# Gate and later-round placement of a mixture-of-experts stage, moved behind the first expert's up product

## What is computed

```python
for e in range(16):                       # 16 SwiGLU experts of width 512
    h = silu(t @ w1[e]) * (t @ w3[e])     # up
    out += gates[:, e:e+1] * (h @ w2[e])  # down
```

## Time and profile before

| | us |
|---|---|
| median of 3 runs | 1329.08 |
| profiled execution, its time | 1333.09 |
| its span (first to last instruction) | 1331.4 |
| PE busy | 910.7 (68%) |
| DVE busy | 416.6 (31%) |
| POOL busy | 312.1 (23%) |
| ACT busy | 171.4 (13%) |
| bytes moved by DMA | 275.74 MB, 207 GB/s over the span |

### The profile page before, as it was taken

How to read it: one execution, slowest core, us unless ns; L and a number is a source line. 1 busy time by engine, 2 the same in 40 slices (tenths; PEclk the granted TensorE clock), 3 DMA queues, 4 the chain that set the end, 5 groups by cost and what they waited for, 6 DMA issues and landing times.

```text
span 1331.4 us, 13807 instructions
## 1 busy us (share of the span) xinstructions
PE 910.7 (68%) x4042; PEld 460.2 (35%) x4043; DVE 416.6 (31%) x887; ACT 171.4 (13%) x316; POOL 312.1 (23%) x568
## 2 busy tenths in 40 slices
PE   3934405969677876873698886669778778766770
PEld 2723302454222322221465653335363223222220
DVE  1599977161111111112412432220531111111114
ACT  1100003030111100100112322111020011101000
POOL 0499995001111211112300001210011211111110
PEclk9967756957999888897699988889859988988886
DMA  7318201085998999995703011217334799999982
GB/s 219 96 32 284 94 0 32 0 290 170 363 363 285 317 361 367 375 373 178 263 12 119 9 36 59 64 36 277 133 102 143 254 356 367 367 378 364 359 298 87
DMA packets 131710, 275.74 MB, mean 207 GB/s; under 512 B 8940, under 2 KB 35800, under 8 KB 131653
## 3 DMA queue, kind: packets, MB, share of 16 engines
q1 hardware_dynamic: 116400, 236.11, 49.7%
q0 software_dynamic: 7808, 20.98, 6.7%
q10 hardware_dynamic: 7461, 18.13, 4.1%
HBM read 257.88 MB, written 18.03 MB: 207 GB/s over the span
## 4 chain that ended last, share of the span: by engine, by line
PE 36%; DMA 33%; DVE 9%; POOL 7%; issue 7%; SPq 3%; ACT 2%; ACTq 2%; POOLq 0%; DVEq 0%
DMA w<-in_e_w 31%; POOL dbuf L420 6%; PE bank L847 5%; PE bank L783 3%; PE wide L847 3%; PE bank L857 3%; PE wide L783 2%; PE bank L1447 2%; PE bank L1348 1%; PE wide L819 1%; PE bank L1327 1%; DVE w L970 1%; PE bank L1499 1%; SPq L1188 1%; DMA x_tok<-sum_rows 1%
## 5 line engine op out<-in xcount | busy, mean ns | idle before, releaser
L847 PE MATMUL bank<-w,dbuf 128*64 128x512 f32 x576 | 145.8, 664 | 44.7 <-DMA w<-in_e_w 42.0
L847 PE MATMUL wide<-w,dbuf 128*64 128x512 f32 x512 | 131.6, 673 | 52.5 <-DMA w<-in_e_w 52.5
L857 PE MATMUL bank<-w,dbuf 128*64 128x512 f32 x544 | 137.2, 649 | 20.5 <-DVE dbuf L1129 19.5
L963 DVE SCALAR_TENSOR_TENSOR w<-w,dw_T x240 | 133.1, 630 | 0.0
L389 POOL TENSOR_TENSOR spare<-spare 1x1 f32<-1x1 f32 x68 | 15.7, 230 | 466.0 <-DVE dbuf L1136 402.8
L847 PEld LDWEIGHTS bank<-w,dbuf 128*64 128x64 f32 x576 | 44.6, 153 | 142.8 <-issue 129.7
L847 PEld LDWEIGHTS wide<-w,dbuf 128*64 128x64 f32 x512 | 41.0, 155 | 142.6 <-issue 138.9
L455 POOL DMA_DIRECT2D w<-in_cache_kpe x64 | 35.4, 553 | 220.9 <-PE bank L1502 174.0
L1136 DVE COPY dbuf<-bank 64x512 f32<-64x512 f32 x64 | 44.0, 688 | 135.7 <-PE bank L857 135.3
L857 PEld LDWEIGHTS bank<-w,dbuf 128*64 128x64 f32 x544 | 45.3, 149 | 87.2 <-issue 85.8
L420 POOL TENSOR_TENSOR dbuf<-dbuf 128x128 f32<-128x128 f32 x124 | 75.0, 605 | 0.3
(11 more groups left out here) (298 smaller groups left out, 1224.1 us busy)
## 6 DMA issues: line engine op xcount, KB each, us to landing
w<-in_e_w SPq DMA_DIRECT2D x96, 2048.0 KB, 14.2
dbuf<-in_a_w_pw SPq DMA_DIRECT2D x16, 512.0 KB, 5.2
w<-in_cache_ckv SPq DMA_DIRECT2D x64, 128.0 KB, 2.3
dbuf<-in_a_w_pw SPq DMA_DIRECT2D x1, 4096.0 KB, 15.1
dbuf<-in_b_w_o SPq DMA_DIRECT2D x1, 4096.0 KB, 12.6
dbuf<-in_b_w_uq SPq DMA_DIRECT2D x1, 3072.0 KB, 12.1
x_rows<-x_tok ACTq DMA_DIRECT2D x4, 512.0 KB, 3.0
dbuf<-in_b_w_dq SPq DMA_DIRECT2D x1, 2048.0 KB, 28.6
```

Of the source, the lines that this page charges most:

```text
L847: last = nc.tensor.matmul(bank[n * C:(n + 1) * C], x[:, k], w[:, n, k], start=(k == 0), stop=(k == KD - 1))
L857: last = nc.tensor.matmul(bank[n * C:(n + 1) * C], h[:, k], w[:, k, n * 512:(n + 1) * 512], start=(k == 0), stop=(k == 3))
L963: V.scalar_tensor_tensor(chunk(acc, j, 0, SEQ), chunk(ext, j, k, SEQ), w, chunk(acc, j, 0, SEQ), ALU.mult, ALU.add).then_inc(tap, 1)
```

## The change

The five calls of line 823 to 827 become a function `gates()`, called behind the first expert's up product. To have a place for the call, expert 0 is written out ahead of the loop and expert 13 behind it; the loop covers experts 1 to 12 with the buffers' parity exchanged. No other engine's program changes.

```diff
--- before.py
+++ after.py
@@ -820,11 +820,14 @@
                 return last
 
             to_slots(B[7][0:C, 0:E], hot, lambda n, m: right[0:m, n, 0]).then_inc(r_slot, 1)
-            pe.wait_ge(r_gated, l + 1)
-            for q in range(CHUNKS):
-                last = to_slots(B[3][0:C, 2 * E * q:2 * E * (q + 1)], hot if q == 0 else hot_more[:, q - 1],
-                                lambda n, m: right[0:m, n].rearrange("p a e -> p (a e)"))
-            last.then_inc(r_gates, 1)
+            def gates():
+
+                pe.wait_ge(r_gated, l + 1)
+                for q in range(CHUNKS):
+                    last = to_slots(B[3][0:C, 2 * E * q:2 * E * (q + 1)], hot if q == 0 else hot_more[:, q - 1],
+                                    lambda n, m: right[0:m, n].rearrange("p a e -> p (a e)"))
+                last.then_inc(r_gates, 1)
+
             g0 = E * l
 
             def turn_rows(bank, src, n):
@@ -890,17 +893,28 @@
 
             n = 16 * (E // 2) * l
             turn(g0, 0, n + 16)
-            with pe.Fori(0, (E - 2) // 2) as it:
+            do_up(g0, 0, 2 * n + 32)
+            gates()
+            turn(g0 + 1, 1, n + 16)
+            pe.wait_ge(cnt_set, l + 1)
+            do_hidden(g0)
+            do_down(g0, 0, n + 16)
+            further(0, 0)
+            with pe.Fori(0, (E - 4) // 2) as it:
                 for s in range(2):
-                    e = it * 2 + s
-                    do_up(e + g0, s, it * 32 + (2 * n + 32))
-                    turn(e + (g0 + 1), 1 - s, it * 16 + (n + 16 + 16 * s))
-                    if s == 0:
-                        pe.wait_ge(cnt_set, l + 1)
+                    e = it * 2 + (s + 1)
+                    do_up(e + g0, 1 - s, it * 32 + (2 * n + 32 + 32 * s))
+                    turn(e + (g0 + 1), s, it * 16 + (n + 32))
                     do_hidden(e + g0)
-                    do_down(e + g0, s, it * 16 + (n + 16))
-                    further(e, s)
-            n += 16 * (E - 2) // 2
+                    do_down(e + g0, 1 - s, it * 16 + (n + 16 + 16 * s))
+                    further(e, 1 - s)
+            n += 16 * (E - 4) // 2
+            do_up(g0 + E - 3, 1, 2 * n + 32)
+            turn(g0 + E - 2, 0, n + 32)
+            do_hidden(g0 + E - 3)
+            do_down(g0 + E - 3, 1, n + 16)
+            further(E - 3, 1)
+            n += 16
             do_up(g0 + E - 2, 0, 2 * n + 32)
             turn(g0 + E - 1, 1, n + 16)
             do_hidden(g0 + E - 2)
```

## The result

The changed kernel took 1346.42 us (median of 7 runs, 1340.87 to 1351.54), the kernel before 1334.58 us (median of 7, 1327.82 to 1337.15). The ratio is 1.011 (95% interval 1.0079 to 1.0141), which is not formed from the two medians: slower by 11.8 us by the medians and by 14.7 us by the ratio. A second measurement of the same kernel gave 1.0064 (1.0035 to 1.0094), 8.5 us, and 11.4 us between the medians. The forecast was +14.2 us.

What follows compares the result with a forecast made beforehand. PE's serial work between slots and expert 1's up product was taken to bound each stage's start, before the weight stream; +8.5 and +5.7 us, together +14.2, on 1329.08 gave 1343.3 us, range 1334 to 1349.

Steps and rivals of the forecast that it cites:

- What bounds: Both expert stages: PE's work between the slots and expert 1's up product is paid in full; weight loads move with it.
- Rival 3: Expert 2's weight landing ends last anyway and absorbs the change: no change, 1329.1 us; chance 0.07.
- rival 4: The 60 products fall into PE's wait between up product and hidden turn: -7.6 us, 1321.5 us; chance 0.03.
- The turn: Turn of expert 0's rows starts earlier, limited by the gather's landing: -2.4 us in layer 0, -5.2 in layer 1.
- The up product: Expert 0's up product stays at 10.07 us; 1.5 us less if the clock rises after 3.05 us.
- Rival 2: Clock not granted in the up product, as PE idles before it: +4.0 us a layer, 1351.3 us; chance 0.06.
- The 60 products: Behind the up product they take 7.3 us a layer, the higher clock lasting 2.9 us; bounds 5.6 and 9.2.
- rival 1: Clock stays high behind the up product, gates 5.6 us a layer, down product not cooled: +5.6, 1334.7 us; chance 0.12.
- The tail: Behind the 60 products: VectorE's lines 1.2 us, table load and loop entry 1.5, silu and gating 1.65 as before.
- Hidden turn and down product: Expert 0's hidden turn and down product run colder after the small products: +0.7 and +0.2, +0.9 us a layer.
- Sum: Later start of expert 1's up product: +8.5 us in layer 0, +5.7 in layer 1, together +14.2 us.
- The base: Median of the runs, 1329.08 us, 4.0 below the profiled 1333.09; the increment was put on it, giving 1343.3 us.

Runs made afterwards that it cites:

- the new loop: Kernel before with expert 0 ahead of PE's loop, expert 13 behind, parity exchanged, but the 60 products still ahead of the first turn: 1334.02 us, ratio 1.0008.
- the early silu: Changed kernel with expert 0's silu and the copy of expert 1's turned rows ahead of ScalarE's count wait: 1344.86 us, ratio 1.0087 to the kernel before.
- the doubled products: Changed kernel with each layer's 60 products run twice behind the up product: 1372.06 us, ratio 1.0266 to the kernel before.
- the split kernel: Against the kernel before: three calls ahead of the first turn, one before and one after the hidden turn, silu ahead of the count wait: 1326.72 us, ratio 0.9937.
- the run with the products in between: Changed kernel's loop form, with the 60 products between expert 0's turn and its up product: 1342.55 us, ratio 1.0053 to the kernel before.

## Why the prediction was right or wrong

*What bounds:* right. What was put into the start interval came out in the measured time, to within some 4 us (the new loop and the early silu had 4 us less in it and were not measurably faster). Rival 3 (the weight stream absorbs it) is out by the doubled products, and rival 4 (the products fall into waiting time) by the 2.92 us in which PE still waits behind them. In the split kernel the products do fall into waiting time, but there by design.

*The turn:* -2.4 and -5.2 were forecast; measured from the slot products it came 1.75 and 5.3 us earlier. The size in layer 0 depends on the gather, which took 7.2 us from issue to landing there and not 6.6. That the wait costs by itself is shown by the run with the products in between.

*The up product:* unchanged at 10.07 forecast. It took 9.1 and 9.9 us, 8.6 and 9.9 in the second trace: in layer 0 it was 0.9 to 1.4 us shorter, by less time at the lower clock, as it also was in the third trace of before (9.26). Rival 2 did not happen.

*The 60 products:* mis-sized. I had 7.3 us, with the clock falling after 2.9; it lasted through nearly all of them, and they took 5.91 and 5.79 us. That is near the 5.6 got from the ratio of 0.61, and not the 3.7 estimated in rival 1. The fall I had read in the earlier trace rows came after 2.9 us in which PE stood idle for half (0.85 and 0.61 us), and I took it over to products without gaps. Rival 1 was right in this and wrong in the rest, as the down product was cold nevertheless.

*The tail:* 1.2 + 1.5 + 1.65 = 4.35 us forecast, 4.28 measured in each layer. The table load began 0.19 us after the count, and silu 0.02 us after the load. The Trainium skill, "ScalarE: Activation LUTs", What ACT_TABLE_LOAD costs, has about 1.38 us of drain with each switch to another table set. Here nothing of that size is seen, and the measurement decides. Nor is it seen where ScalarE was busy until the load, as in the trace of before, whose load begins at 309.46, 0.02 us behind this copy of the turned rows:

```profile
308.84 0.60 ACT L639 ACTIVATE dbuf<-bank 128x512 f32<-128x512 f32 x1 [18.25 <-PE bank L834]
```

The run with the early silu took 2.15 us of the 4.28 away. That load and silu were in PE's path is thus shown, not only argued.

*Hidden turn and down product:* +0.9 a layer forecast against the trace of before. Hidden turn 0.97 and 0.98 against 0.59; down 5.58 and 6.02 against 5.30 and 5.22. Summed that is +0.7 and +1.2, right against that trace; but it was one in which the down product of before was cold in both layers. Against a warm one (3.65) it is +2.3 and more.

*Sum:* the terms give +8.5 and +5.7; the start intervals of the same two traces +6.4 and +4.2. The forecast increment of 14.2 us was thus 3.6 too large in its own terms. Of that the 60 products are 2.9 and the up product of layer 0 is 0.9. In the other direction, the rest of the profiled execution, which I had put at nothing, was 7.9 us longer (attention and experts, cause open). That the increment still lies at the measured 11.8 (medians) to 14.7 (ratio) is in part luck: the two errors have opposite signs.

*The base:* the step that failed. I put the increment on 1329.08, the median of three runs. The kernel before measured 1334.58 us (median of seven) together with the changed one, 5.5 us more, and 1332.2 to 1334.6 later. The changed kernel's median of 1346.42 is 3.1 us above the forecast 1343.3. By the ratio it is 1334.58 x 1.011 = 1349.3 us, just outside the range of 1334 to 1349. On a base of 1334.58 the same increment gives 1348.8. The profiled execution was at 1333.09, nearer to the true middle than the median of the three, and I had read the 4.0 us between them as a surcharge of that execution. With runs that spread over 7 us in three, a forecast should have stood on both and its range should have carried the base's own uncertainty.

## What to carry to other kernels

Work that seems to stand ahead of its turn may cover a transfer: before moving it, look up when the transfer lands, for the cover goes and the work is paid again behind. A stage that is bound by a stream is still bound by one engine's serial work until the stream starts; put small products into the waits of that engine, in portions that fit, and let each consumer wait only for the portion that it reads. A wait at a loop's entry also holds back what stands at the head of the loop without being in the source, here a table load of 1.28 us. And a base from three runs that spread over 7 us carries an error of several us into every forecast put on it, here 5.5.

## What the runs showed of the hardware

- Small float32 products (64 columns of weights, 32 moving) cost 0.153 us per instruction at the lower clock (60 in 9.20 us) and 0.097 at the higher one (60 in 5.79). Sixty in a row behind the up product kept the higher clock almost to their end; 120 in a row did not (15.37 us).
- An instruction with 512 moving columns and 64 columns of weights lasts 0.59 us at the higher clock. With outputs alternating between two halves of a bank 16 of them took 3.65 us, with all outputs in one half 8 did.
- The clock after light work differed from trace to trace of the same kernel: a down product of 16 instructions took 5.30 us in two traces of before and 3.65 in a third, at the same place. Such events may be part of the spread of 10 to 20 us between executions: of twelve runs of the new loop the fastest, 1327.84 us, had a mean granted clock of 0.839 and the slowest, 1346.56, one of 0.821. How large a part is not shown.
- ScalarE's table load began 0.19 us after the wait that held it and silu followed at once, 1.5 us in all; nothing like a drain was to be seen.
